# Layer norm of a 31-tap convolution on Trainium2: channel tiles added on VectorE before the averaging product

## The reference

```python
def layer_norm(x, g, b):
    xf = x.astype(jnp.float32)
    mu = jnp.mean(xf, axis=-1, keepdims=True)
    xc = xf - mu
    var = jnp.mean(xc * xc, axis=-1, keepdims=True)
    y = xc * lax.rsqrt(var + EPS) * g.astype(jnp.float32) + b.astype(jnp.float32)
...
    c = glu[..., :D_CONV] * jax.nn.sigmoid(glu[..., D_CONV:])
    c = causal_depthwise_conv(c, cf_dw_w) + cf_dw_b
    c = jax.nn.silu(layer_norm(c, cf_ln_g, cf_ln_b))
    return jnp.concatenate([o, c], axis=-1) @ w_out
```

## Time and profile before

| | |
|---|---|
| median of three executions | 2585.26 us (2584.73 to 2587.01) |
| the profiled execution, its own time | 2584.61 us |
| its span, first to last instruction | 2582.8 us |
| TensorE (PE) busy | 2557.4 us, 99% |
| VectorE (DVE) busy | 1660.2 us, 64% |
| ScalarE (ACT) busy | 1346.5 us, 52% |
| HBM traffic | 181 GB/s over the span |

### The profile page before, as it was taken

The page is one execution under the profiler, slowest core; times in us unless marked ns, Lnnn a source line. Parts: engine busy times, 40 slices in busy tenths (PEclk is TensorE's granted clock), DMA queues, the critical chain, the costliest instruction groups (busy, mean ns, idle before and its releaser), DMA issues.

```text
span 2582.8 us, 33847 instructions
## 1 busy us (share of the span) xinstructions
PE 2557.4 (99%) x13780; PEld 2156.5 (83%) x13780; DVE 1660.2 (64%) x2128; ACT 1346.5 (52%) x1907; POOL 0.2 (0%) x4
## 2 busy tenths in 40 slices
PE   9999999999999999999999999999999999999998
PEld 7878888888888888887888888888888888888887
DVE  8686565655655567668788967544556655665566
ACT  6565554444444446568866665544454444444444
POOL 0000000000000000000000000000000000000000
PEclk9999999999999999999999999999999999999999
DMA  6533666556555655555454437544555555556554
GB/s 228 171 132 136 226 220 204 187 189 196 195 188 188 195 195 173 194 177 174 138 188 142 149 130 254 179 146 147 193 192 190 192 196 190 188 193 196 190 187 144
DMA packets 235041, 470.77 MB, mean 182 GB/s; under 512 B 8235, under 2 KB 17158, under 8 KB 233478
## 3 DMA queue, kind: packets, MB, share of 16 engines
q1 hardware_dynamic: 234134, 467.04, 54.8%
q10 hardware_dynamic: 752, 1.58, 0.2%
HBM read 462.30 MB, written 6.29 MB: 181 GB/s over the span
## 4 chain that ended last, share of the span: by engine, by line
PE 49%; DVE 1%; ACT 0%; issue 0%; DVEq 0%
PE ps L1267 10%; PE ps L1269 10%; PE ps L1268 10%; PE ps L1306 9%; PE ps L1305 5%; PE ps L1659 1%; PE ps L1814 1%; PE ps L1839 1%; PE ps L1338 0%; PE ps L1713 0%; PE ps L1597 0%; PE ps L1588 0%; PE ps L1750 0%; PE ps L1640 0%; PE ps L1736 0%
## 5 line engine op out<-in xcount | busy, mean ns | idle before, releaser
L2652 DVE TENSOR_TENSOR WL<-Wt,WH 128x1024 fp32r<-128x1024 f32 (+1 forms) x861 | 1037.6, 1210 | 707.8 <-ACT WH L1894 657.0
L1894 ACT ACTIVATE WH<-Wt 128x1024 fp32r<-128x1024 f32 (+1 forms) x861 | 894.5, 1046 | 769.8 <-PE ps L1269 509.0
L1267 PE MATMUL ps<-WH,XT 128*128 128x512 f32 (+1 forms) x1184 | 470.8, 398 | 0.7 <-DVE WL L2652 0.4
L1267 PE MATMUL ps<-WH,HT 128*128 128x512 f32 (+2 forms) x1176 | 457.0, 389 | 3.3 <-DVE WL L2652 3.3
L1269 PE MATMUL ps<-WH,XT 128*128 128x512 f32 (+1 forms) x1184 | 459.4, 388 | 0.0
L1268 PE MATMUL ps<-WL,XT 128*128 128x512 f32 (+1 forms) x1184 | 459.0, 388 | 0.0
L1269 PE MATMUL ps<-WH,HT 128*128 128x512 f32 (+2 forms) x1176 | 451.5, 384 | 0.0
L1268 PE MATMUL ps<-WL,HT 128*128 128x512 f32 (+2 forms) x1176 | 451.1, 384 | 0.0
L1306 PE MATMUL ps<-XT,WH 128*128 128x512 f32 x960 | 336.5, 394 | 0.0
L1306 PE MATMUL ps<-HT,WH 128*128 128x512 f32 x960 | 336.5, 394 | 0.0
L1305 PE MATMUL ps<-HT,WL 128*128 128x256 f32 x960 | 266.6, 278 | 0.0
(11 more groups left out here) (404 smaller groups left out, 1884.4 us busy)
## 6 DMA issues: line engine op xcount, KB each, us to landing
Wt<-in_mlp_w SPq DMA_DIRECT2D x128, 1024.0 KB, 5.1
Wt<-in_w_up SPq DMA_DIRECT2D x64, 1024.0 KB, 5.3
Wt<-in_w_down SPq DMA_DIRECT2D x64, 1024.0 KB, 4.9
Wt<-in_w_in SPq DMA_DIRECT2D x53, 1024.0 KB, 5.1
Wt<-in_w_out SPq DMA_DIRECT2D x32, 1024.0 KB, 5.0
Wt<-in_xa_wk SPq DMA_DIRECT2D x16, 1024.0 KB, 5.0
Wt<-in_xa_wv SPq DMA_DIRECT2D x16, 1024.0 KB, 5.0
Wt<-in_xa_wq SPq DMA_DIRECT2D x16, 1024.0 KB, 5.0
```

Source lines behind the costliest of these rows:

```text
L1267: pe.matmul(o, xh, wh, start=start, stop=False)
L1894: act.activation(m.WH[:, i % NR, 0:2 * w], m.Wt[:, slot % NW, h * 2 * w:(h + 1) * 2 * w], ACT.Copy).then_inc(*up("wsplit.a", i))
L2652: dve.tensor_tensor(m.WL[:, i % NR, 0:2 * w], m.Wt[:, slot % NW, h * 2 * w:(h + 1) * 2 * w], m.WH[:, i % NR, 0:2 * w].bitcast(F32), SUB).t ...
```

## The change

The eight tiles are added to one on VectorE before the product, for the mean and for the mean of squares: `fold` adds four tiles to four, two to two, one to one (128x1024, 128x512, 128x256), into `LNA`. Each product is then one matmul instead of eight. `gen_ln` gets two more steps, `cln_fold` ahead of `cln_mean` and `cln_fold_squares` ahead of `cln_var`, so that every later step of the layer norm stands two halves later. `cln_square` also waits for the mean's product, which now reads `LNA`.

```diff
     def gen_ln():
+        p.do("cln_fold")
+        yield
         b = p.bank()
         p.do("cln_mean", b)
         yield
...
         p.do("cln_square", 1)
+        yield
+        p.do("cln_fold_squares")
         yield
         p.do("cln_var", *p.banks(1))
         yield
...
     def cln_mean(b):
         for s in freed(b):
             on.wait_ge(*s)
-        for c in range(8):
-            on.wait_ge(*at("cconv.v", "added", 58 + c // 4))
-            t = pe.matmul(m.bank(b)[:, 0:256], m.cst("mean"), m.AC[:, c, :], start=c == 0, stop=c == 7)
-        t.then_inc(*up("cln.t", "mean"))
+        on.wait_ge(*at("cln.v", "folded", 0))
+        pe.matmul(m.bank(b)[:, 0:256], m.cst("mean"), m.LNA[:, 0, :], start=True, stop=True).then_inc(
+            *up("cln.t", "mean"))
...
     def cln_var(b):
         for s in freed(b):
             on.wait_ge(*s)
-        on.wait_ge(*at("cln.a", "square", 1))
-        for c in range(8):
-            t = pe.matmul(m.bank(b)[:, 0:256], m.cst("mean"), m.LNA[:, c, :], start=c == 0, stop=c == 7)
-        t.then_inc(*up("cln.t", "var"))
+        on.wait_ge(*at("cln.v", "folded", 1))
+        pe.matmul(m.bank(b)[:, 0:256], m.cst("mean"), m.LNA[:, 0, :], start=True, stop=True).then_inc(
+            *up("cln.t", "var"))
...
     def cln_square(g4):
         cs = slice(4 * g4, 4 * g4 + 4)
         on.wait_ge(*at("cln.v", "centered", 1))
+        on.wait_ge(*at("cln.t", "mean"))
...
+    def fold(src, n):
+
+        dve.tensor_tensor(m.LNA[:, 0:4, :], src[:, 0:4, :], src[:, 4:8, :], ADD).then_inc(*up("cln.v"))
+        on.wait_ge(*last("cln.v"))
+        dve.tensor_tensor(m.LNA[:, 0:2, :], m.LNA[:, 0:2, :], m.LNA[:, 2:4, :], ADD).then_inc(*up("cln.v"))
+        on.wait_ge(*last("cln.v"))
+        dve.tensor_tensor(m.LNA[:, 0, :], m.LNA[:, 0, :], m.LNA[:, 1, :], ADD).then_inc(*up("cln.v", "folded", n))
+
+    @named
+    def cln_fold():
+        for k in (58, 59):
+            on.wait_ge(*at("cconv.v", "added", k))
+        on.wait_ge(*at("cconv.a", 58))
+        fold(m.AC, 0)
+
+    @named
+    def cln_fold_squares():
+        for g4 in range(2):
+            on.wait_ge(*at("cln.a", "square", g4))
+        fold(m.LNA, 1)
```

## The result

The changed kernel takes 2591.94 us (median of nine executions, 2590.85 to 2595.96) against 2585.51 for the kernel before, timed beside it: a ratio of 1.0027, 95% interval 1.0018 to 1.0035. That is 6.4 us slower, and clear of the 0.2% that I called the limit. The forecast was 2589.0 with "no change" as the likeliest case; the time lies just inside the range.

The account below looks back on a forecast made before the run. TensorE, busy 2557 of 2583 us, was taken to bound the kernel. -6.0 (matmuls) + 0 (additions) + 7.4 (stop) + 2.7 (clock) = +4.1 us gave 2589.4, stated as 2589.0, range 2584.5 to 2592.0.

Parts of the forecast that it names:

- no change: Whole kernel: time within about 0.2% (5.2 us) of before, between 2580.1 and 2590.4 us; chance 67%.
- The removed matmuls, -6.0: At the layer norm's mean and variance: 28 fewer matmul instructions on TensorE save 6.0 us (5.9 to 6.3).
- The first fold "meets" TensorE, 0: At the mean: VectorE's additions end at 1490.0, TensorE arrives at 1490.1; 0 to 0.3 us of waiting, taken as 0.
- The stop at half 510, +7.4: Before w_out_2's first half: TensorE idles until VectorE's late `cln_low 0` is done; 7.4 us, between 5.2 and 8.5.
- The walk: From `d_out`'s last eviction at 1544.95: instruction orders of ScalarE and VectorE followed forward, putting half 510's start at 1569.35.
- One of the signs named: In the layer norm's tail: `cln_mul 1` was to end near the end of half 508.
- The clock, +2.7: At the half 510 stop: TensorE's clock falls to 0.50 and slow matmuls afterwards cost 2.7 us, range 0 to 3.65.
- The lower bound of 1.8: Clock loss after the stop: half the 3.6 us slow stretch that followed TensorE's last restart at the program's start.
- the middle that I took: Clock loss after the stop: 2.7 us, between 1.8 and 3.65 us read from the program's start.
- the last sentence of part three: On SP's queue: two 2 MB loads ahead of one more weight load make its first half wait 0 to 1 us, taken as 0.
- Slower: Rival: low clock outlasts the stop, over w_out_2's first three halves, costing half its length; over 2590.4 us; 29%.
- The range: Whole kernel: 2584.5 us, the low end if the clock stays, up to 2592.0, for a longer low clock or stop.

Follow-up runs that it names:

- merged: The change with two steps taken out of the layer norm's tail (scale joined with affine, abs with log): 2579.89 us, 6.1 us under the kernel before.
- keep_warm: The change plus 15 matmuls of 256 columns, sums unread, on TensorE between half 509 and half 510: 2590.33 us, 4.3 us over the kernel before.
- kv_late: The change with one empty step ahead of the two 2 MB loads: 2590.27 us, 4.3 us over the kernel before.
- merged_one: The change with one step taken out of the layer norm's tail (scale joined with affine): 2583.84 us, 1.7 us under the kernel before.
- no_steps: The change with each addition in the same step as the product needing it, so no step is added: 2592.64 us against 2585.56 before.

## Why the prediction was right or wrong

- **The removed matmuls, -6.0: right.** 6.06 by the traces, 6.1 by merged.
- **The first fold "meets" TensorE, 0: right.** In the change's trace the additions end at 1491.71 + 0.42 = 1492.13 and the product starts at 1492.28, with no wait shown:

```profile
1491.71 0.42 DVE L3270 TENSOR_TENSOR LNA<-LNA 128x256 f32<-128x256 f32 x1
```
```profile
1492.28 0.70 PE L1591 MATMUL ps<-LNA,CST 128*128 128x256 f32 x2
```

- **The stop at half 510, +7.4: right**, 7.39, and by its mechanism. The walk put split 507 at 1549.6 and `cln_low 0` at 1568.1 in the clock of before; the traces are 3.87 apart at the border, which makes 1545.73 and 1564.23. They stand at 1545.74 and 1564.17. One of the signs named was off by a half: `cln_mul 1` ends at 1557.88, at the end of half 509 and not of half 508. The walk itself had it there, behind split 510.
- **The clock, +2.7: right in kind, too large in the profiled execution.** It fell within the stop and cost 1.57 behind it; keep_warm, which has no fall there, gains 1.7 by the traces and 2.1 by the medians. The lower bound of 1.8, the stretch after an unbroken restart, was nearer than the middle that I took.
- **The step that failed is the last sentence of part three: "0 to 1 us, I take 0" for the two 2 MB loads ahead of one more weight load.** It cost 2.0 us in the trace and 2.1 in the medians. The landing was not later than I had thought, 14.3 us where I had said 18. The deadline was wrong: I asked when half 524 needs its weights, but on VectorE the eviction of half 521 is queued behind split 524, and TensorE needs that eviction ahead of half 523, one half earlier. In kv_late, with the load back in its place, the wait is gone. I had followed the data of the late load and not what stands behind the waiting instruction.
- **The chances.** "Slower" had 29% with the mechanism of a clock that stays low over 7.6 us. It came out slower, but that mechanism is not why: the low stretch under work was 3.2 us. The sum of the four terms, corrected by the traces, is -6.1 + 7.4 + 1.6 + 2.0 = +4.9, where I had +4.1: the missing wait of 2.0 and the clock, 1.1 too large, partly cancelled. Against it stand +5.2 by the traces and +6.4 by the medians. The 1.2 us between these two are 2.1 us that lie ahead of the delta rule's first product, less the 0.9 by which the profiled execution of before was under its median. My sum had no term for that, and the fall at 155 us, the larger part of it, is not the change's.
- **The range.** That 2591.94 lies 0.06 us inside it is in part luck. Its upper end stood for a clock that stays low for longer, or for a longer stop. Neither came; the time got there by the late load and by what lies ahead of the delta rule's first product.

## What to carry to other kernels

When a chain of background work is lengthened by a step, look at its far end: what matters is not whether the new work is hidden but whether the last result still comes ahead of the consumer, and what then stands between them in each engine's order. Walk the instruction order of every engine from the last point that the bounding engine sets. For a late transfer, the deadline is that of everything queued behind the instruction that waits for it. Here the cure for a step added at the front was to join two steps of one engine at the back, which turned 6.4 us of loss into 6.1 of gain.

## What the runs showed of the hardware that I had not expected

A stop of 2.65 us (merged_one) was enough for TensorE's clock to fall to 1.2 GHz, and it fell at about 1561.9, 1 us after TensorE had begun to work again; behind the stop of 3.9 us in no_steps it also fell some 1.2 us after the restart. I had looked only for a fall inside the stop. In both it came back after some 3.4 us; in the change it was low for 6.8 us and came back 3.2 us after TensorE had begun to work again. The low stretch cost about 1.6 us in merged_one and 1.57 in the change. A window of merged_one:

```profile
1562.00:1564.00 2.00, 2.00 (x6) 1.56 (x5) 2.00 (x3) 0.00 (x0) 0.00 (x0) 0.50 0.76 225
```

Still less can be enough. The wait of 1.6 us at 154 us was followed by a fall in six of ten profiled executions; in the change's the clock fell at 155.6, 0.8 us after the restart. In the other four it stayed at 1.00 behind the same wait. So the length of a wait alone does not tell whether the clock falls, and two profiled executions of one kernel can differ by 1.6 us for this reason.

A short stop therefore costs more than its length where the clock falls: with the low stretch behind it 2.65 us became 4.3 in merged_one, and in no_steps 3.9 became 5.6 and 4.4 became 7.3.
